# Gated sparse attention in fp32: seven-unit steps over one long and one short query tile, weights scaled before the turn, three branches summed in one PSUM bank

## The reference

```
s_cmp = q . k_cmp            p_cmp = masked_softmax(s_cmp, cmp_end <= pos)
s_sel = q . k_sel            p_sel = masked_softmax(s_sel, kpos <= tq)
s_w   = q . k_win            p_w   = masked_softmax(s_w, causal)
o = g0 * (p_cmp @ v_cmp) + g1 * (p_sel @ v_sel) + g2 * (p_w @ v_win)     # g0..g2: sigmoid gates per head and token
```

## Time and profile before

| | before |
|---|---|
| median of 3 runs | 1652.23 us (1651.34 to 1652.46) |
| profiled execution | 1654.73 us, span 1652.7 us |
| PE busy | 1588.4 us, 96% |
| DVE, ACT, POOL busy | 68%, 43%, 15% |
| first score of the attention | 700.06 us |
| first product of the output projection | 914.02 us |

### The profile page before, as it was taken

One profiled execution on the slowest core, in us unless ns is written; L12 is line 12 of the kernel. 1 busy time (PEld: TensorE's weight loads), 2 busy tenths in 40 slices (PEclk: granted clock), 3 DMA queues, 4 the chain that ended last, 5 costly groups with the idle time before them and its releaser, 6 DMA issues.

```text
span 1652.7 us, 23027 instructions
## 1 busy us (share of the span) xinstructions
PE 1588.4 (96%) x8475; PEld 1332.0 (81%) x8475; DVE 1124.8 (68%) x1719; ACT 714.1 (43%) x1319; POOL 244.5 (15%) x205
## 2 busy tenths in 40 slices
PE   4898999999999999899999899999999999999998
PEld 3687888888888978899899798888888897776677
DVE  6698778889897743366766477565634644688785
ACT  3332552323223733266666453231314443678651
POOL 0122113232231000122322002111100001010110
PEclk9899999999999999989999999999999999999999
DMA  9565357576774134300000134444423322112201
GB/s 334 203 218 178 100 181 264 192 258 235 237 249 140 55 104 153 107 1 2 1 0 0 52 121 167 153 159 153 141 89 102 104 79 77 52 55 74 76 1 51
DMA packets 106738, 203.27 MB, mean 123 GB/s; under 512 B 6025, under 2 KB 11414, under 8 KB 106646
## 3 DMA queue, kind: packets, MB, share of 16 engines
q1 hardware_dynamic: 106646, 202.01, 35.8%
HBM read 199.90 MB, written 2.10 MB: 122 GB/s over the span
## 4 chain that ended last, share of the span: by engine, by line
PE 76%; DVE 12%; ACT 4%; issue 3%; DMA 3%; POOL 1%; SPq 0%; DVEq 0%; POOLq 0%; ACTq 0%
PE PS L2011 41%; PE PS L1968 16%; PE PS L2337 4%; DVE MACC L1234 4%; DVE WL L1200 3%; PE PS L2318 2%; PE PS L2301 2%; PE PS L2300 1%; ACT WH L705 1%; PE PS L2332 1%; POOL MROW L484 1%; PE PS L2253 1%; PE PS L2478 1%; DMA MRAW<-in_ada_w_dram 1%; PE PS L2041 1%
## 5 line engine op out<-in xcount | busy, mean ns | idle before, releaser
L705 ACT ACTIVATE WH<-RAW 128x2048 fp32r<-128x2048 f32 (+1 forms) x112 | 210.0, 1886 | 363.2 <-DMA RAW<-in_ff_w_in_dram 220.1
L1200 DVE TENSOR_TENSOR WL<-RAW,WH 128x2048 fp32r<-128x2048 f32 (+1 forms) x107 | 276.0, 2600 | 127.7 <-ACT WH L705 127.7
L484 POOL PARTITION_ALL_REDUCE MROW<-MACC x30 | 142.2, 4740 | 597.7 <-DVE MACC L1234 597.7
L2011 PE MATMUL PS<-WH,HIDh 128*128 128x512 f32 (+1 forms) x576 | 219.7, 381 | 5.7 <-DVE HIDl L1518 4.9
L2011 PE MATMUL PS<-WL,HIDh 128*128 128x512 f32 (+1 forms) x576 | 219.3, 381 | 0.0
L2011 PE MATMUL PS<-WH,HIDl 128*128 128x512 f32 (+1 forms) x576 | 219.1, 380 | 0.0
L2011 PE MATMUL PS<-HTh,WH 128*128 128x512 f32 (+1 forms) x520 | 202.5, 389 | 0.6 <-DVE WL L1200 0.6
L2011 PE MATMUL PS<-HTl,WH 128*128 128x512 f32 (+1 forms) x520 | 202.4, 389 | 0.0
L2011 PE MATMUL PS<-HTh,WL 128*128 128x512 f32 (+1 forms) x520 | 202.3, 389 | 0.0
L1234 DVE SCALAR_TENSOR_TENSOR MACC<-MRAW,CS,MACC 128x512 f32<-128x512 f32 x182 | 136.9, 752 | 9.0 <-DMA MRAW<-in_ada_w_dram 0.9
L2011 PEld LDWEIGHTS PS<-WH,HIDh 128*128 128x128 f32 x576 | 109.7, 190 | 26.8 <-issue 6.0
(11 more groups left out here) (322 smaller groups left out, 3166.6 us busy)
## 6 DMA issues: line engine op xcount, KB each, us to landing
MRAW<-in_ada_w_dram SPq DMA_DIRECT2D x46, 1024.0 KB, 7.4
RAW<-in_ff_w_in_dram SPq DMA_DIRECT2D x32, 1024.0 KB, 5.5
RAW<-in_ff_w_out_dram SPq DMA_DIRECT2D x32, 1024.0 KB, 5.1
RAW<-in_w_in_dram SPq DMA_DIRECT2D x16, 1024.0 KB, 5.4
MRAW<-in_w_ada_dram SPq DMA_DIRECT2D x12, 1024.0 KB, 8.8
RAW<-in_a_w_in_dram SPq DMA_DIRECT2D x8, 1024.0 KB, 9.7
MRAW<-in_kv_ada_w_dram SPq DMA_DIRECT2D x8, 1024.0 KB, 6.3
RAW<-in_kv_w_dram SPq DMA_DIRECT2D x6, 1024.0 KB, 5.2
```

The lines of the kernel that those rows point to most:

```text
L484: pool.partition_all_reduce(MROW[:], MACC[:], P, RADD).then_inc(m_red, 1)
L705: act.activation(WH[:, wslot(u), 0:width(u)], RAW[:, u % 4, 0:width(u)], ACT.Copy).then_inc(w_hi, 1)
L1200: dve.tensor_tensor(WL[:, u % 4, 0:width(u)], RAW[:, u % 4, 0:width(u)], WH[:, wslot(u), 0:width(u)].bitcast(F32), ALU.subtract).then_inc( ...
L2011: mm = pe.matmul(po, a, b_, start=(k == 0 and i == 0), stop=(k == KT - 1 and i == len(ops) - 1), skip_group_check=len(ops) > 3)
```

## The change

The whole attention stage is written anew.

- **Steps.** A step S is one pair of heads and two query tiles: a short one (qt = S % 2) and a long one (qt = 3 - S % 2), so 640 keys in every step. There are 16 steps of 7 units, 112 units, written out without a hardware loop. Unit 0 is the compressed branch of two tiles and two heads, units 2 and 5 are the short tile of one head with both branches side by side, units 1, 3, 4 and 6 the long tile with one branch and one head.
- **Compressed scores.** The high and low part of the compressed keys stand side by side in KC, so one product a tile and head with 64 columns gives both halves, and DVE adds them (the first of three operations of `negmax`). ACT takes the exponential of 128 columns in one, and DVE the sums (`cmp_sums`).
- **Weights scaled untransposed.** The coefficients of a whole step are computed once (`coefs_of`, 12 columns), and the weights are multiplied with them before they are turned: unit 0, 3 and 6 on DVE (`weights`), 1, 2, 4 and 5 on POOL, six operations a step, in place in PB.
- **One bank.** V is now PE's weights (64 columns) and the turned weights are streamed (128 columns): the result comes out turned, and all three branches add up in the same columns, head 0 in partitions 0 to 63, head 1 in 64 to 127. The compressed branch is one product with 128 weight columns, for which POOL puts the compressed values a second time at another place (VC, block diagonal). OM, OA, the sums on POOL and `turn_out` are gone; `out_hi` and `out_lo` come once a step, 256 columns each.
- **Lags and rings.** `turn` is 12 slots behind `scores`, the copies 14, `values` 16, and `values` handles three units at once. PB has 12 rows, PT 5, the score banks go from 4 to 3 and the banks of turned weights from 2 to 3.
- POOL stages two pairs of heads before the stage, clears VC and PTC, and copies VC once DVE has written it; PE's first score waits for that copy.

```diff
-    PB = at("PB", [P, 4, 512], F32, o_rb)
...
+    PB = [at(f"PB{i}", [P, 512], F32, o_rb + 2048 * i if i < 4 else o_mraw + 2048 * (i - 4)) for i in range(12)]
...
-    OM, OA = scratch("OM", [P, 2, 6 * HD]), scratch("OA", [P, 2, P])
+    KC = scratch("KC", [P, GROUPS, 2, 32], F32R)
+    KCh, KCl = KC[:, :, 0, :], KC[:, :, 1, :]
+    VC = scratch("VC", [P, GROUPS, 2 * HD])
...
+    PT = [scratch(f"PT{i}", [P, 512]) for i in range(5)]
+    PBC = [scratch(f"PBC{i}", [P, P]) for i in range(2)]
+    PTC = [scratch(f"PTC{i}", [P, 2 * P]) for i in range(2)]
...
-        sp.wait_ge(a_om, GROUPS * BLOCKS)
+        sp.wait_ge(a_t, UNITS)
...
+        pool.memset(VC[:], 0.0).then_inc(vc_zero, 1)
+        for i in range(2):
+            pool.memset(PTC[i][:], 0.0).then_inc(vc_zero, 1)
...
+            S, i, pair, qts, blk, br, e, L = unit(u)
+            if i == 1:
+                pool.wait_ge(a_rc, 3 * S + 3)
+            for at_, br_ in parts(u):
+                w, c_ = PB[row(u) % 12][:, at_:at_ + L], 12 + 12 * (S % 2) + 6 * blk + 3 * e + 1 + br_
+                pool.tensor_scalar(w, w, SM[:, c_:c_ + 1], None, ALU.mult).then_inc(a_ps, 1)
+            pool.wait_ge(*scaled(u))
...
+        for pair in range(2):
+            for stage in (stage_hi, stage_lo):
+                for e in range(2):
+                    stage(pair, e)
+        pool.wait_ge(kc_r, 3)
+        pool.tensor_copy(VC[32:64, :, HD:2 * HD], VC[0:32, :, 0:HD]).then_inc(vc_copies, 1)
+        for S in range(SUPER):
+            pair = (S + 3) // 2
+            staged = S % 2 == 1 and pair < KT
+            if staged:
+                pool.wait_ge(a_sc, 2 * PER * (pair - 1))
+                for e in range(2):
+                    stage_hi(pair, e)
+            for i in (1, 2, 4, 5):
+                weights(PER * S + i)
+            if staged:
+                for e in range(2):
+                    stage_lo(pair, e)
         for _ in range(6):
             mod()
 
...
-    BLOCKS = 8
-    UNITS = 5 * BLOCKS
-    LAG = 10
+    SUPER, PER = 2 * KT, 7
+    UNITS = PER * SUPER
+    TURN_LAG, COPY_LAG, VALUES_LAG = 12, 14, 16
...
-        b, k = u // 5, u % 5
-        return b, b // TT, b % TT, (k + 1) // 2, (k - 1) % 2, (P * (b % TT + 1) if k else CMP)
+        S, i = u // PER, u % PER
+        qts = (S % 2, 3 - S % 2)
+        if i == 0:
+            return S, i, S // 2, qts, None, None, None, 32
+        if i in (2, 5):
+            return S, i, S // 2, qts, 0, None, i // 5, P * (qts[0] + 1)
+        return S, i, S // 2, qts, 1, i // 4, i // 3 - i // 4, P * (qts[1] + 1)
...
-        return u % 5 in (0, 2, 4)
+        return u % PER in (0, 1, 2, 4)
...
+        def exp(u):
+            S, i, pair, qts, blk, br, e, L = unit(u)
+            act.wait_ge(a_nm, u + 1)
+            if i == 0:
+                act.activation(PBC[S % 2][:], PBC[S % 2][:], ACT.Exp, scale=-1.0).then_inc(a_ex, 1)
+                return
+            if S >= 2:
+                act.wait_ge(a_t, u - 2 * PER + 1)
+            sums, w = 12 + 12 * (S % 2) + 6 * blk + 3 * e + 1, weights_of(u)
+            for j, (at_, br_) in enumerate(parts(u)):
+                c_ = 2 * (u % 4) + j
+                a = act.activation(w[:, at_:at_ + L], PS[:, u % 3, at_:at_ + L], ACT.Exp, bias=SM[:, c_:c_ + 1],
+                                   accum_out=SM[:, sums + br_:sums + br_ + 1])
...
+        act.wait_ge(vc_zero, 3)
+        for t in range(UNITS + VALUES_LAG + 1):
+            if 0 <= t - COPY_LAG < UNITS and by_act(t - COPY_LAG):
+                copy(t - COPY_LAG)
+            if t < UNITS:
+                exp(t)
+            S, at_ = (t - VALUES_LAG - PER) // PER, (t - VALUES_LAG) % PER
+            if at_ == 0 and 0 <= S < SUPER:
+                out_hi(S)
+            if t == UNITS + 6:
+                act.wait_ge(a_sc, UNITS)
                 hi(2 * n.chunk)
-
-        over_groups(act, slot)
-        act.wait_ge(a_pv, GROUPS * UNITS)
-        hi(2 * n.chunk + 1)
+            if t == UNITS + COPY_LAG:
+                act.wait_ge(a_pv, 3 * SUPER - 2)
+                hi(2 * n.chunk + 1)
...
+                    dve.wait_ge(a_t, u - 2 * PER + 1)
+                two = PS[:, u % 3, 0:2 * P].rearrange("p (r k c) -> p r k c", r=4, k=2)
+                w = four(PBC[S % 2][:])
+                dve.tensor_reduce(w, two.rearrange("p r k c -> p r c k"), AX_X, ALU.add).then_inc(a_mx, 1)
+                dve.wait_ge(a_mx, 2 * S + 1)
+                dve.tensor_reduce(SM[:, 8:12], w, AX_X, ALU.max).then_inc(a_mx, 1)
+                dve.wait_ge(a_mx, 2 * S + 2)
+                dve.scalar_tensor_tensor(out=w, in0=SM[:, 8:12, None].to_broadcast([P, 4, 32]), scalar=FLOOR, in1=w,
+                                         op0=ALU.max, op1=ALU.subtract).then_inc(a_nm, 1)
...
+            if br is None:
+                m, v = SM[:, c_:c_ + 2], PS[:, u % 3, 0:2 * L].rearrange("p (h c) -> p h c", h=2)
...
+                m, v = SM[:, c_:c_ + 1], PS[:, u % 3, 0:L]
+            dve.tensor_reduce(m, v, AX_X, ALU.max, negate=True).then_inc(a_nm, 1)
...
+            w, c_ = weights_of(u)[:, 0:L], 6 * blk + 3 * e + 1 + br
+            dve.tensor_scalar(w, w, sums_of(S)[:, c_:c_ + 1], None, ALU.mult).then_inc(a_pd, 1)
...
+        for t in range(UNITS + VALUES_LAG + 2):
+            if 0 <= t - COPY_LAG < UNITS and not by_act(t - COPY_LAG):
+                copy(t - COPY_LAG)
+            if t < UNITS:
+                negmax(t)
+            S = (t - 2) // PER
+            if (t - 2) % PER == 0 and S < SUPER:
+                cmp_sums(S)
+            S, at_ = (t - 8) // PER, (t - 8) % PER
+            if 0 <= S < SUPER:
+                if at_ == 0:
+                    coefs_of(S)
+                    weights(PER * S)
+                elif at_ in (1, 4):
+                    weights(PER * S + 3 * (at_ // 4 + 1))
+            S = (t - VALUES_LAG - PER - 1) // PER
+            if (t - VALUES_LAG - 1) % PER == 0 and 0 <= S < SUPER:
+                out_lo(S)
+            if t == UNITS + 7:
                 lo(2 * n.chunk)
...
+            if i == 0:
+                for r in range(4):
+                    pe.matmul(PS[:, u % 3, HD * r:HD * r + HD], queries(qts[r // 2], r % 2),
+                              KC[:, g].rearrange("p k c -> p (k c)"), start=(r == 0), stop=False, skip_group_check=True)
+                where = PS[:, u % 3, 0:2 * P].rearrange("p (t h c) -> p t h c", t=2, h=2)[:, :, :, 0:32]
+                mask = MCM[:, qts[0]:qts[1] + 1:qts[1] - qts[0], None, :].to_broadcast([P, 2, 2, 32])
+            else:
+                if br is None:
+                    out_, of = PS[:, u % 3, 0:2 * L].rearrange("p (b c) -> p b c", b=2), slice(0, 2)
+                    where, mask = out_[:, :, L - P:L], MD[:, None, :].to_broadcast([P, 2, P])
...
+                    out_, of = PS[:, u % 3, 0:L], br
+                    where, mask = out_[:, L - P:L], MD[:]
+                for k in (KDh, KDl):
+                    pe.matmul(out_, queries(qts[blk], e), k[:, of, g, 0:L], start=(k is KDh), stop=False,
+                              skip_group_check=True)
+            pe.matmul(where, IDB[:], mask, start=False, stop=True, skip_group_check=True).then_inc(a_sc, 1)
+
+        def turn(u):
+            pe.wait_ge(*scaled(u))
+            if u >= 3:
+                pe.wait_ge(*copied(u - 3))
+            step, rows_ = (P, P) if u % PER else (HD, HD)
+            for i in range(wide(u) // P):
+                mm = pe.transpose(PS[0:rows_, 3 + u % 3, P * i:P * i + P], weights_of(u)[:, step * i:step * i + step],
+                                  IDENT[:])
+            mm.then_inc(a_t, 1)
...
+            if i == 0:
+                pe.wait_ge(*copied(u))
+                if S >= 2:
+                    pe.wait_ge(a_ol, S - 1)
+                mm = pe.matmul(PS[:, 6 + S % 2, 0:2 * P], VC[:, g, :], PTC[S % 2][:], start=True, stop=False,
+                               skip_group_check=True)
...
+                for v in (u - 2, u - 1, u):
+                    pe.wait_ge(*copied(v))
+                for v in (u - 2, u, u - 1):
+                    S, i, pair, qts, blk, br, e, L = unit(v)
+                    for at_, br_ in parts(v):
+                        for kt in range(qts[blk] + 1):
+                            c_ = at_ + P * kt
+                            mm = pe.matmul(head(blk, e), VT[:, br_, kt, HD * g:HD * g + HD], turned_of(v)[:, c_:c_ + P],
+                                           start=False, stop=(br_ == 1 and kt == qts[blk]), skip_group_check=True)
...
+        for t in range(UNITS + VALUES_LAG):
+            if t < UNITS:
+                scores(t)
+            if 0 <= t - VALUES_LAG < UNITS and (t - VALUES_LAG) % PER in (0, 3, 6):
+                values(t - VALUES_LAG)
+            if 0 <= t - TURN_LAG < UNITS:
+                turn(t - TURN_LAG)
```

361 lines of the change are left out of this document (124 added, 237 removed).

## The result

| | before | after |
|---|---|---|
| median (the last measurement beside each other, 4 runs each) | 1652.03 us | 1608.36 us (1605.46 to 1610.40) |
| profiled execution | 1654.73 us, span 1652.7 | 1608.31 us, span 1606.6 |
| first score to first product of the projection | 213.96 us | 171.97 us |
| a pair of heads in mid-stage | 25.46 us | 20.07 us |

The ratio is 0.9735 with a 95% interval of 0.9718 to 0.9752: 43.7 us faster, where 31 were forecast.

A forecast was written before the change was run, and what follows sets the result against it. PE, busy for 96% of the span, was taken as the bound; 27.7 (pairs) - 3.5 (start) + 3.7 (end) + 3.4 (clock) = 31 us saved, giving 1624 profiled and a median of 1621, range 1609 to 1641.

The forecast's parts named there:

- The excursion to 64-column weights: Each call of values on PE loses 0.28 us changing weight shape; two calls a step cost 1.1 a pair.
- rival D: In values, the two heads' products overlap by one MATMUL at each change of half: 5 us less, 1616; chance 0.08.
- the term of the values: PE's values MATMULs go from 0.112 to 0.107 us each through narrower weights: gain 0.4 us a pair.
- pair of heads, 8 times: PE's work in mid-stage falls 3.5 us a pair, 25.46 to 22.0: gain 27.7 us for the stage.
- start, with POOL's copy of VC: At the stage's start, waiting for the copy and slots with little PE work cost 3.5 us.
- end: After the last values, ACT's copy and DVE's subtraction take 1.3 us instead of 5.0: gain 3.7.
- clock at the projection: With shorter PE idle, the clock stays at 2.4 GHz at the output projection: gain 3.4 us, or nothing.
- rival C: Half clock lasts through the first 18 slots (+4) and returns at the output projection (+3.4): 1629; chance 0.12.
- The loads of the others: Work per 11.0 us step: DVE about 9.1, ACT 8.4, POOL 6.6 with 512 columns at 1.0; all hidden.
- rival B: POOL's scaling in weights becomes the bound, 16.5 us a step: 59 longer, 1711; slower past 12.9 a step; chance 0.04.
- A: DVE's and ACT's chain, not their load, sets the step at 12 us: +16, 1637; chance 0.21.
- E: No difference: the gains and a chain as in A, but at 12.8 us a step; chance 0.03.

The follow-up runs named there:

- kernel with the heads in turn: Kernel after, with the products of the two heads alternating one by one within a call of values: 1602.09 us, ratio 0.9691.
- kernel with one half: Kernel after, with both heads' products in values written to partitions 0 to 63: 1625.68 us, ratio 0.9839.
- the run with the pause: Kernel after, with VectorE's last subtraction of the attention repeated six times, one waiting for the other, before the projection: 1614.10 us, ratio 0.9769.
- the later split: Kernel before, with VectorE's first subtraction of the projection's weights moved behind the attention's last operation: 1655.05 us in one run.

## Why the prediction was right and wrong

**What was right.** The bound: PE stays busy through all of a pair, and the gain is PE's own work. The parts of its steady state, apart from one, measured as costed. The compressed product of 256 columns: 0.43 expected for its two MATMULs, 775.72 to 776.15 is 0.43. The short scores: 0.11 each. The excursion to 64-column weights: 0.28 expected. From the mask to the values it is 0.21 (778.57 to 778.78), to the compressed product, which keeps the shape, 0.12 (775.60 to 775.72); the first gap is 0.160 for 0.109, the way out 0.203 for 0.109, and the first transpose behind it 0.05 longer: together 0.29. Within a half the starts are 0.109 apart, for a forecast of 0.107. With the overlap taken away, the pair takes 22.25 for a forecast of 22.0. The Trainium skill's page TensorEngine Tiling (Array Packing), Key Properties, lets different tiles multiply in parallel; the starts 6 ns apart in different halves, and 109 ns apart in the same, agree.

**The step that failed** is the size of rival D, and with it the 0.107 for each MATMUL in the term of the values ("**Gain 0.4**"). The forecast of 1621 had this overlap at nothing, and the rival let one start overlap at each change of half, 48 x 0.107 = 5 us. Measured is 0.36 to 0.38 a change, from three kernels with none, four and six changes a pair: 48 x 0.36 = 17 us, since the second half begins about three products before the first is through. The term of the values was thus -2.2 a pair off. No row of the trace of before shows two neighbours with different halves, so the price could not be read; but the two ends could have been bounded. "One start" was a guess in the middle, and the far bound (each half streams by itself, and a call lasts as long as its longer half) was not worked out. In calls of three units the shorter half has 6 or 8 MATMULs, 14 a step on average, so it is 14 x 0.109 x 16 = 24 us, and the range would have reached to 1597. The kernel with the heads in turn shows that this is the bound: its pair is 22.25 - 19.27 = 2.98 us below that of the kernel with one half, 24 us for eight.

**The other terms of the sum.**

| term | forecast | measured |
|---|---|---|
| pair of heads, 8 times | 3.5 x 8 = 27.7 | 5.39 x 8 = 43.1 |
| start, with POOL's copy of VC | -3.5 | -5.3: the stage's 171.97 less 8 x 20.07 and 1.1 at the end is 10.3 where it was 5.3; 0.3 for the copy ahead of it |
| end | 3.7 | 3.9 |
| clock at the projection | 3.4 | 2.7 (first product to the next idle time, before and after) |

The measured terms add up to 44.4 us, and the medians are 43.7 apart. Two of the errors go the other way than the overlap, by 1.8 and 0.7 us, so that the total is nearer to the forecast than the term of the values is.

The start cost 1.8 us more. In its slots of scores PE runs at the half clock and waits for the exponential: the half clock lasts 13.7 us in place of 10.2. That is rival C's direction, but not to the end of the 18 slots, and at a smaller price than its 4. In the profiles of the other kernels with the new attention the stretch is 6.8 to 17.1 us long. The first two steps go with it, in kernels with the lags of the kernel after or one slot less: 14.2 to 14.3 us where it is 6.8, 15.1 where it is 13.7, 16.5 to 16.6 where it is 17.1. What sets it is not settled; the run with the pause shows that the same program has it in different lengths.

**The loads of the others** were too high for two engines and too low for one: DVE 9.1 a step forecast, 8.4 measured (100.46 us in 731.00 to 851.42, twelve steps); ACT 8.4 and 6.5; POOL 6.6 and 7.7. GpSimd's 512 columns took not 1.0 but 1.61 in the mean, from the profile's groups by form:

```profile
L550 POOL TENSOR_SCALAR PB<-PB,SM 128x256 f32<-128x256 f32 x32 | 31.8, 1003 | 1.5
L550 POOL TENSOR_SCALAR PB<-PB,SM 128x512 f32<-128x512 f32 x16 | 25.7, 1606 | 22.5 <-DVE SM L1734 21.7
L550 POOL TENSOR_SCALAR PB<-PB,SM 128x128 f32<-128x128 f32 x32 | 21.3, 677 | 1.5
...
L550 POOL TENSOR_SCALAR PB<-PB,SM 128x384 f32<-128x384 f32 x16 | 20.2, 1263 | 15.6 <-DVE SM L1734 14.7
```

A part of it is VectorE: POOL's 128 columns take 0.60 us by themselves (the median) and 0.90 in the five places where a whole scaling of 512 columns on DVE (0.48 us) runs beside them, which is the blocking that rival B feared, at 0.3 us a time. All this cost nothing at 77% of a step, and the cover that the prediction named, the lag of 12 slots, is what hides it: at 10 slots it shows at once, and with 2.6 us a step more POOL is the bound. Rivals A, B and E did not happen; the runs show that B was nearer than its chance of 0.04 suggests (a step on POOL past some 9.5 us, by the estimate above, and not 12.9, costs time), though it would have needed far more to make the kernel slower than before.

## What to carry to other kernels

When products write fewer than all of PE's output columns, see whether two streams can go to different halves: started in turn, with the same count in each half and in each call, two products cost the time of one, and the order of a loop is worth several us at no other cost. When a profile has no row for the neighbours that a change makes, put the far bound into the range too, not one guess in the middle. Before a step's sums are drawn into one call, count what the ring behind it leaves free: saving a call's ends is nothing if all copies have to wait for it.

## What the runs showed of the hardware that was not expected

- Two 64-column products of different output halves (partitions 0 to 63 and 64 to 127) start 6 to 7 ns apart; in the same half they start 109 ns apart. Where the program does not start them in turn, the second half's begin about three products early.
- GpSimd's multiplication by a column of scalars takes 0.68, 1.00, 1.26 and 1.61 us for 128, 256, 384 and 512 columns on 128 partitions, some 0.31 us for each 128 columns (means of the kernel after; they hold what VectorE delays). That is slower than its subtraction of two operands in `stage_lo`, 1.27 us for 512 columns on 64 partitions, from which the forecast had taken its 1.0.
- One GpSimd operation beside VectorE's 2048-column subtraction of two operands in SBUF took 2.33 us for 0.45, and in the kernel after 2.51 for 0.92.
- PE's pause at the end of the attention, of 3.8 to 4.0 us, came with 6.8 us at half the clock (1.2 GHz) in all three traces that have it (before 3.79, the longer pause 3.83, the later split 3.99); one of 1.1 us did not.
